# A mixer block's first experts: router and norm per token from raw rows, a gather split by four experts, and two more places for weights

## The reference, cut to what matters

```
x = x + mod_x[2] * merge(o_x, g_x, hy_x)          # merge ends in "@ w_out", 1024 x 1024
hn = rmsnorm(x, norm_ffn_g) * (1 + scale) + shift # scale, shift = mod[4], mod[3], one number per feature
aff = softmax(hn @ w_router)                      # 256 tokens x 16 experts
vals, idx = top_k(aff.T, 32)                      # each expert takes its 32 best tokens
xs = hn[idx]                                      # 16 experts x 32 slots x 1024
hid = silu(xs @ w_gate) * (xs @ w_up)             # each expert 1024 x 1024
x = x + mod_x[5] * scatter_add((hid @ w_down) * vals)
```

## Time and profile before

| | before |
|---|---|
| median of 3 runs | 1888.96 us (1887.69 to 1889.4) |
| profiled execution | 1888.17 us, span 1886.3 us |
| PE busy | 1576.7 us (84%) |
| DVE, ACT busy | 480.5 us (25%), 328.2 us (17%) |
| HBM read | 492.06 MB |
| mean granted clock of TensorE | 0.915 of full speed |

### The profile page before, as it was taken

How to read it: one execution, slowest core, us unless ns; L and a number is a source line. 1 busy time by engine, 2 the same in 40 slices (tenths; PEclk the granted TensorE clock), 3 DMA queues, 4 the chain that set the end, 5 groups by cost and what they waited for, 6 DMA issues and landing times.

```text
span 1886.3 us, 18196 instructions
## 1 busy us (share of the span) xinstructions
PE 1576.7 (84%) x7592; PEld 852.2 (45%) x7592; DVE 480.5 (25%) x998; ACT 328.2 (17%) x675; POOL 0.2 (0%) x4
## 2 busy tenths in 40 slices
PE   6999997765555565679797899999798978999996
PEld 3657777311111111156566644433575667443434
DVE  5112442200000000044563322111335633221213
ACT  1323111100000000013232212111112222122211
POOL 0000000000000000000000000000000000000000
PEclk9999999877888778689898999999998988999999
DMA  9215426499999999952321399999114213899970
GB/s 387 123 55 219 173 95 262 167 429 428 428 428 428 428 428 428 428 209 76 147 90 45 134 383 384 393 410 425 69 45 155 92 67 134 355 387 398 405 326 24
DMA packets 35306, 494.40 MB, mean 262 GB/s; under 512 B 3920, under 2 KB 4176, under 8 KB 4688
## 3 DMA queue, kind: packets, MB, share of 16 engines
q1 hardware_dynamic: 34640, 491.08, 63.3%
q10 hardware_dynamic: 576, 2.05, 0.3%
HBM read 492.06 MB, written 1.05 MB: 261 GB/s over the span
## 4 chain that ended last, share of the span: by engine, by line
PE 70%; DMA 21%; DVE 6%; ACT 2%; issue 1%; DVEq 0%
PE PS L521 26%; DMA A<-ring_d 20%; PE PS L1203 12%; PE PS L1226 6%; PE PS L789 3%; PE PS L1079 3%; PE PS L1188 3%; PE PS L1241 3%; PE PS L526 3%; PE PS L533 2%; PE PS L1068 2%; PE PS L905 1%; PE PS L587 1%; PE PS L1032 1%; DVE A L1818 1%
## 5 line engine op out<-in xcount | busy, mean ns | idle before, releaser
L521 PE MATMUL PS<-A 128*128 128x256 f32 (+6 forms) x1984 | 525.6, 423 | 21.5 <-DVE A L1638 7.2
L521 PEld LDWEIGHTS PS<-A 128*128 128x128 f32 (+2 forms) x1984 | 372.5, 195 | 164.6 <-issue 103.0
L789 PE MATMUL PS<-A 128*32 128x512 f32 x1536 | 260.0, 814 | 171.9 <-DMA A<-ring_d 170.4
L1203 PE MATMUL PS<-A 128*64 128x512 f32 x1024 | 226.8, 595 | 0.1
L789 PEld LDWEIGHTS PS<-A 128*32 128x32 f32 x1536 | 51.4, 130 | 369.1 <-DMA A<-ring_d 227.3
L1203 PEld LDWEIGHTS PS<-A 128*64 128x64 f32 x1024 | 71.6, 137 | 133.0 <-issue 132.8
L1226 PE MATMUL PS<-A 128*64 128x512 f32 x512 | 116.9, 599 | 0.0
L1625 DVE TENSOR_TENSOR A<-A,PS 128x512 f32<-128x512 f32 x8 | 5.5, 690 | 396.5 <-PE PS L789 396.5
L526 PE MATMUL PS<-A 128*128 128x128 f32 (+1 forms) x396 | 64.9, 299 | 39.0 <-DVE A L1839 8.5
L526 PEld LDWEIGHTS PS<-A 128*128 128x128 f32 (+1 forms) x396 | 49.0, 153 | 84.4 <-issue 53.2
L2003 DVE TENSOR_TENSOR A<-A,PS 128x256 f32<-128x256 f32 x32 | 13.5, 423 | 226.7 <-ACT A L2473 226.7
(11 more groups left out here) (288 smaller groups left out, 1137.7 us busy)
## 6 DMA issues: line engine op xcount, KB each, us to landing
A<-ring_d SPq DMA_DIRECT2D x228, 2048.0 KB, 12.6
A<-ring_d SPq DMA_DIRECT2D x2, 1312.0 KB, 16.4
A<-ring_d SPq DMA_DIRECT2D x2, 1280.0 KB, 13.9
A<-xT_d SPq DMA_DIRECT2D x2, 1024.0 KB, 9.2
A<-pf_d SPq DMA_DIRECT2D x4, 512.0 KB, 20.2
A<-p_d SPq DMA_DIRECT2D x1, 1278.5 KB, 5.7
A<-p_d ACTq DMA_DIRECT2D x1, 1232.0 KB, 5.9
A<-cT_d SPq DMA_DIRECT2D x1, 1024.0 KB, 20.8
```

The lines of the kernel that those rows point to most:

```text
L521: ins = g.matmul(out, l, r, start=n == 0, stop=n == len(pairs) - 1)
L789: ins = g.matmul(ps[32 * e:32 * e + 32, :], rows_of(kk, e), wv[:, kk % 2, e, :], start=kk == 0, stop=kk == 7)
L1203: ins = g.matmul(ps[64 * s:64 * s + 64, :], XS2[u % 2][:, kk, c:c + 64], wv[:, kk % 4, s, :], start=kk == 0, stop=kk == 7)
```

## The change

Five things are changed together, all between the output product and the end of the first experts.

- **Router from raw rows.** During the output product, PE turns each pair of chunks of the new X token-major (not normalised) and multiplies them with router weights that were scaled by `MA[:, 4]` beforehand (`rows`, `wr`). The shift's part of the logits, `MA[:, 5] @ w_router`, is a row that is the same for all tokens (`ROUT`). DVE takes mean and variance per token from the turned rows; from these comes the reciprocal root per token, and the logits are raw logits times it plus `ROUT`.
- **Norm token-wise.** ACT scales the turned rows HT by the reciprocal root per token (`normed`). Gain and shift are applied to the gathered slots, when they leave PSUM for XS (`slots` on ACT and DVE).
- **Gather by four experts.** The gather runs for four experts at a time: for the first four ahead of their weights, for the others inside the experts of the group before. So does the turning of PV.
- **Selection.** The first max reads the turned affinities from PSUM, without a copy; the scan takes a broadcast column of ones, without a memset.
- **Two more places.** YE (free once the attention's output `o` is done) and the region of M and T (free once the output product is done) each take one block of expert weights, once: blocks 23 and 27. Eight blocks of expert weights can lie ready. The ring of six goes on after that.

The diff, cut to its core. The order of the steps and the table of places:

```
-    + [("out", 0), ("out", 1)]
+    + [("wr",), ("out", 0), ("out", 1), ("rows", 0), ("out", 2), ("rows", 1), ("out", 3), ("rows", 2), ("rows", 3)]
...
-SLOTS = [0, 1, 2, 3] * 2 + [0, 1, 2] * 4 + [4, 5, 6, 0, 1, 2] * 16 + ([4, 5, 0, 1, 2] * 2 + [4, 5, 0, 1, 2, 6] * 8) * 2
...
+YE_SLOT, MT_SLOT = 7, 8
+SLOTS = [0, 1, 2, 3] * 2 + [0, 1, 2] * 4 + [4, 5, 6, YE_SLOT, 0, 1, 2, MT_SLOT] + [4, 5, 6, 0, 1, 2] * 14 + [4, 5, 6, 0] \
+    + ([1, 2, 4, 5, 0] * 2 + [1, 2, 4, 5, 0, 6] * 8) * 2
```

On PE:

```
+            def wr():
...
+                g.wait_ge(*at("ma", 1))
+                group(ps[:, 0:16], [(bc(MA[:, 5, k:k + 1], [128, 128]), w_rt[:, k, :]) for k in range(8)]).then_inc(*full("wr"))
...
+            def rows(b):
...
+                g.wait_ge(*at("out", b))
+                for ti in range(2):
+                    for j in range(2):
+                        ins = turn(ps[:, ti * 256 + j * 128:ti * 256 + j * 128 + 128], X[:, 2 * b + j, ti * 128:(ti + 1) * 128])
+                ins.then_inc(*full("htt", b))
+                g.wait_ge(*at("wr"))
+                for k in (2 * b, 2 * b + 1):
+                    for ti in range(2):
+                        ins = g.matmul(bank("router")[:, ti * 16:(ti + 1) * 16], X[:, k, ti * 128:(ti + 1) * 128], w_rt[:, k, :],
...
-            column_sum(T, 8, ("esum",), (("esq", 0), ("esq", 1)))
...
+            def slots(x):
...
+                g.wait_ge(*at("pm", x > 0))
+                for q in range(2):
+                    ps = fresh("xs", x, q)
                     for j in range(4):
...
+                        c = (4 * q + j) * 128
+                        ins = group(ps[:, j * 128:(j + 1) * 128], [(HT[:, ti, c:c + 128], PM[:, ti, 4 * x:4 * x + 4, :].rearrange("p e j -> p (e j)"))
+                                                                   for ti in range(2)])
+                    ins.then_inc(*full("xs", x, q))
...
+            slots(0)
             for x in range(4):
...
+                if x < 3:
+                    slots(x + 1)
+                weights_turned(x)
                 g.wait_ge(*at("hidt", x, 1))
```

On DVE, behind the last turned rows, and where PM is built:

```
+            for ti in range(2):
+                ins = v.bn_aggr(MV1[:, ti, :], BN1[:, ti, :, :])
...
+            v.tensor_tensor(MS1, MV1[:, :, 0], MV1[:, :, 0], ALU.mult).then_inc(*out())
...
+            v.tensor_tensor(MS1, MS1, MV1[:, :, 1], ALU.add).then_inc(*out("ms"))
+            v.wait_ge(*at("hstd"))
+            v.reciprocal(RS1, MS1).then_inc(*out("rs"))
...
+            places(0, 4, "pm", 0)
+            slots(0)
+            places(4, 16, "pm", 1)
```

On ACT, in the rows and up to the exp:

```
+            def rows(b):
...
+                if b == 3:
+                    s.wait_ge(*at("ms"))
+                    s.activation(MS1, MS1, ACT.Sqrt, bias=EPS6, scale=1.0).then_inc(*out("hstd"))
+                full("htt", b)
+                s.wait_ge(*at("bn1", b))
+                s.activation(HT[:, :, b * 256:(b + 1) * 256], bank("htt", b).rearrange("p (t c) -> p t c", t=2), ACT.Copy).then_inc(*out("htt", b))
...
+            s.activation(STAT[:, 62:63], EPS5, ACT.Exp, bias=0.0, scale=1.0).then_inc(*out())
+            s.wait_ge(*at("rs"))
+            settle()
+            normed(0)
+            s.wait_ge(*at("lsub"))
             s.activation(AE, AE, ACT.Exp, bias=0.0, scale=1.0).then_inc(*out("aexp"))
```

On SP:

```
+                if SLOTS[i] == YE_SLOT:
+                    q.wait_ge(*at("full", "o", 1))
+                if SLOTS[i] == MT_SLOT:
+                    q.wait_ge(*at("full", "out", 3))
```

More of the change, by code:

```diff
@@ L317, in program @@
         RING = [take(SLOT) for _ in range(NS)]
-        X, H, M, T = [take(8, 256) for _ in range(4)]
+        X, H = [take(8, 256) for _ in range(2)]
+        Mo = mem.top
+        M, T = [take(8, 256) for _ in range(2)]
         STAT, MODo = take(64), mem.top
@@ L759, in ob, with out_ @@
                 ins.then_inc(*full("ob", hp))
[L761 to L763 removed]
+            def wr():
+                ps = fresh("wr")
+                g.wait_ge(*at("ma", 1))
+                group(ps[:, 0:16], [(bc(MA[:, 5, k:k + 1], [128, 128]), w_rt[:, k, :]) for k in range(8)]).then_inc(*full("wr"))
+            def out_(b):
+                if b % 2 == 0:
+                    w, hold["out"] = weights("out", b // 2)
+                    arrived(hold["out"])
+                    hold["outw"] = w.rearrange("p (k n) -> p k n", k=8)
+                ps = fresh("out", b)
@@ L764, in out_ @@
                 g.wait_ge(*at("mix", 1))
                 g.wait_ge(*at("ic", 1, 3))
-                for j in range(4):
-                    across(("out", half * 4 + j), w.rearrange("p (k n) -> p k n", k=8), j * 128, 128, T)
-                finished(i)
+                for j in range(2):
+                    c = (b % 2) * 256 + j * 128
+                    ins = group(ps[:, j * 256:(j + 1) * 256], [(hold["outw"][:, k, c:c + 128], T[:, k, :]) for k in range(8)])
+                ins.then_inc(*full("out", b))
@@ new lines, in out_ @@
+                if b % 2:
+                    finished(hold["out"])
+            def rows(b):
+                if b == 0:
+                    fresh("router")
+                    banks.hold("router")
+                ps = fresh("htt", b)
+                g.wait_ge(*at("out", b))
+                for ti in range(2):
+                    for j in range(2):
+                        ins = turn(ps[:, ti * 256 + j * 128:ti * 256 + j * 128 + 128], X[:, 2 * b + j, ti * 128:(ti + 1) * 128])
[4 more added lines that the diff above has]
+                        ins = g.matmul(bank("router")[:, ti * 16:(ti + 1) * 16], X[:, k, ti * 128:(ti + 1) * 128], w_rt[:, k, :],
+                                       start=k == 0 and ti == 0, stop=k == 7, skip_group_check=True)
+                if b == 3:
+                    ins.then_inc(*full("router"))
+                    banks.release("router")
@@ L779, in tensor, with four_experts @@
             sig.stage = "moe"
-            def four_experts(ps, key, done, rows_of):
+            def four_experts(ps, key, done, rows_of, ready=None):
                 for part in range(4):
@@ L785, in four_experts @@
                     wv = w.rearrange("p (k e n) -> p k e n", k=2, e=4)
+                    if ready:
+                        g.wait_ge(*at(*ready, part // 2))
                     arrived(i)
@@ L2272, in scalar @@
                         .then_inc(*out("hidt", x, half))
+                if x < 3:
+                    slots(x + 1)
+                full("pvt", x)
+                s.activation(PVT[:, x, :], bank("pvt", x)[:, 0:256], ACT.Copy).then_inc(*out("pvt", x))
                 for half in range(2):
```

153 lines of the change are left out of this document (78 added, 75 removed).

## The result

The changed kernel takes 1860.42 us in the median of four runs (1855.19 to 1861.99), the kernel before 1889.18 beside it: a ratio of 0.9839, 95% interval 0.9812 to 0.9866. Single runs of the kernel before lay between 1887.69 and 1894.35 over all series, above 1891 in one of the four beside the changed kernel and in a larger share in the other series, so that ratios of different series carry a difference of their own. The forecast was 1858 in a range of 1853 to 1868. The profiled execution took 1858.97 for a span of 1857.2, 29.2 less than the profiled one of before.

The account below looks back on a forecast made before the run. The prediction took the DMA-bound stream of expert weights, and when it starts, as the limit. 20.7 us (earlier start) + 9.9 (two places) = 30.6, so 1888.17 - 30.6 = 1857.6, forecast 1858 us, range 1853 to 1868 (8 in 10).

Parts of the forecast that it names:

- The bound: At the experts: 88 blocks of weights in 433.67 us, limited by DMA, so what counts is when this stream starts.
- The start: Product's start to first read of expert weights: first read at about 334.5 in place of 355.16, 20.7 us earlier.
- wr: PE ahead of the output product: 8 matmuls of 16 columns, 1.7 to 3.6 us, taken as 2.0, product from 283.2.
- exp's end: ACT's path from the root at 317.15 through copy, table load and scaling: exp done at 320.95.
- softmax to PM: Selection after the softmax's sum: 7.45 us in place of 8.17, without copy and memset, so PM starts at 328.45.
- gather to first read: Gather for four experts from 329.0, 32 records and ACT's copies: first weights read at about 334.5.
- The two places: Ahead of the experts: two blocks of 96 leave the stream, 2 x 4.93 = 9.9 us, both landed by 329.5.
- The gathers in the stream: Three gathers, 3.3 to 7.3 us each, and turning of PV between gate/up and down: cost nothing, under DMA's cover.
- The skill's rules: Table switch 2.66 us on ACT would give 1859; HBM limit of 358 GB/s would give 1856; the trace contradicts both.
- Places without effect: Rival, 8%: the two added places earn nothing, only the earlier start's 20.7 us is left, 1867.5 us.
- an old tie of the first block: Rival, 6%: the experts' first block still waits for something late, only the places pay, 1878.3 us.
- A hold: Rival, 3%: gathers in the stream keep PE from reading blocks; loses beyond 24.6 us each, about 1892 at 36.

## Why the prediction was right, point by point

- **The bound.** Right: the stream's start and its number of blocks set the end. From six places to eight the time between reads falls by 9.7, from eight to nine by 5.1, and with eight it stays within 0.4 of the changed kernel's for anything done ahead of the first read.
- **The start.** Forecast 334.5, measured 335.41. The gap is one offset carried through: wr began 1.2 later than assumed, at 282.37 (a run that was 0.7 later up to there, and PE's wait of 0.90 for MA's last columns, where the old product had waited 0.45). wr itself took 1.9 (15.84 less half of 27.86), 2.0 in the sum. From there the steps hold: two rows 1.25 each; root at 318.09 (317.15); exp's end at 321.74 (320.95); softmax to PM 7.46 (7.45); PM 0.51 (0.5); gather to first read 5.42 (5.5), with the clock at one half for its first part, as the forecast had chosen. That it came so near is in part luck: in the seven other kernels with the new router, the same gather of 32 records and no additional matmuls it took 5.56 to 6.76.
- **The two places.** 9.9 forecast, 9.69 and 9.74 measured, landed at about 326 where 329.5 was the bound. Of the two blocks that wait for the last product matmul (issued from 314.71) one lies in the region of M and T and one in place 2; The prediction has both new places wait for it, but YE's block is issued fourth and doesn't; the count of two is the same.
- **The gathers in the stream.** Cost 0.25 at most, where nothing was forecast: 438.39 without them, 438.64 with them.
- **The sum.** 30.6 forecast; the last read moved by 29.44, the profiled time by 29.2, the median by 28.8. Of the 1.2 in the last read, 0.95 are the late start and 0.2 the two places (9.69, not 9.9).
- **A term that was left out.** wr was priced by its matmuls alone. Its wait, and the clock that falls behind it in most traces (1.7), weren't in the sum; the range had 1.6 for wr's own records at half speed. The profiled execution was one of the two without the fall, which is luck. That the timed runs' median lies 1.5 above the profiled one would fit with it, but isn't shown.
- **The skill's rules.** The changed kernel's table load runs from 318.89 to 320.17 and the next instruction starts at 320.18, so the 2.66 us that the Trainium skill (ScalarE: Activation LUTs, What ACT_TABLE_LOAD costs) gives for a switch are not seen here either: it took 1.3. The stream again ran at 426 GB/s, above the 358 that the Trainium skill (DMA: Bandwidth & Descriptors, Specifications) lists as the limit of HBM for one core.
- **The rivals.** Places without effect and an old tie of the first block are ruled out by the table. A hold cost 0.6 us with five gathers in place of one, and 34.4 with fourteen.

## What to carry to other kernels

When a stage is bound by a stream of weights, ask what has to happen before the first block's place comes free, and how many blocks fit ahead of it: each microsecond and each block counts in full, and independently of the other. Work that is not needed for the first block belongs inside the stream, as long as it holds PE for less time than the other places cover. What stands at the start of a dense run of matmuls can cost more than its own time: behind wr's wait and its 16-column matmuls the granted clock fell to one half in most traces. And judge an edit of a few us by the times in the trace that it can change, not by the total alone.

## What the runs showed that I had not expected

- The old router's 32 records took 4.09 in the trace of before (granted clock 0.86 from 324 to 328) and 6.85 both with the gather split and with the places alone (0.50): this stretch costs 2.8 us more or less by the clock it meets. Whether the spread of the runs of before has this cause isn't shown.
- A wait of 0.90 us and 16-column matmuls at the product's start were followed by a granted clock of one half in seven of nine traces, 1.7 us each; in the other two the same wait was not.
- The work behind the last read took 1078.3 us with the gather split alone and 1088.7 with the additional matmuls, though neither kernel changes anything there. The cause is open.
- Ten records of additional matmuls raised the clock to full and did not keep it: after two waits of 1.22 and 1.02 us it fell in the middle of the gather.
